# Attention output products of the first 128 tokens moved behind a recurrence, and two chunks' products interleaved

## What is computed

```python
def rwkv7_scan(r, w, k, v, a, b):
    # S_t = S_{t-1} diag(w_t) + (S_{t-1} a_t) b_t^T + v_t k_t^T ; y_t = S_t r_t
...
def rwkv7_mixer(...):
    y = rwkv7_scan(r_h, w_h, k_h, v_h, -kk, kk * a_h)
    mean = jnp.mean(y, axis=-1, keepdims=True)
    var = jnp.mean(jnp.square(y - mean), axis=-1, keepdims=True)
    y = ((y - mean) * lax.rsqrt(var + GN_EPS)).reshape(B_, T_, RW_DIM) * ln_w + ln_b
    return (y + bonus.reshape(B_, T_, RW_DIM)) * g

def second_block(x, ...):
    p = rms_norm_2(x, norm_mix_w) @ w_in
    y_mix = jnp.concatenate([rwkv7_mixer(...), fox_mixer(...)], axis=-1)
    x = x + y_mix @ w_out
    return x + hierarchical_moe(rms_norm_2(x, norm_ffn_w), ...)
```

## Time and profile before

| | |
|---|---|
| median of 3 runs | 1439.1 us (1437.99 to 1439.76) |
| the profiled execution, its own time | 1438.01 us |
| its span, first to last instruction | 1435.8 us |
| granted TensorE clock, mean | 0.906 of full speed |
| PE busy | 1078.6 us, 75% |
| DVE busy | 342.6 us, 24% |
| ACT busy | 217.7 us, 15% |
| POOL busy | 65.5 us, 5% |
| HBM read | 461.45 MB |

### The profile page before, as it was taken

How to read it: one execution, slowest core, us unless ns; L and a number is a source line. 1 busy time by engine, 2 the same in 40 slices (tenths; PEclk the granted TensorE clock), 3 DMA queues, 4 the chain that set the end, 5 groups by cost and what they waited for, 6 DMA issues and landing times.

```text
span 1435.8 us, 34660 instructions
## 1 busy us (share of the span) xinstructions
PE 1078.6 (75%) x15426; PEld 774.4 (54%) x15426; DVE 342.6 (24%) x973; ACT 217.7 (15%) x598; POOL 65.5 (5%) x115
## 2 busy tenths in 40 slices
PE   6999999999999798756566656656566656566665
PEld 4776577646887577544444444444444444444443
DVE  2564156312663451111010111111111101111111
ACT  1163116301432121100000000000000000000000
POOL 1100010001011100000000000000000000000000
PEclk9999999999999899988888898898898887888888
DMA  9752245133220499999999999999999999999997
GB/s 287 257 186 72 91 160 192 31 134 118 78 100 4 177 382 428 428 430 430 431 430 430 430 430 430 430 431 431 430 430 431 429 430 430 430 430 430 431 429 319
DMA packets 69024, 463.37 MB, mean 323 GB/s; under 512 B 14789, under 2 KB 18278, under 8 KB 44390
## 3 DMA queue, kind: packets, MB, share of 16 engines
q1 hardware_dynamic: 64784, 459.77, 77.7%
q10 hardware_dynamic: 4182, 2.74, 0.7%
HBM read 461.45 MB, written 1.05 MB: 322 GB/s over the span
## 4 chain that ended last, share of the span: by engine, by line
DMA 54%; PE 9%; issue 1%; ACT 0%; DVE 0%; POOLq 0%; DVEq 0%; POOL 0%
DMA work_region<-in_exp_w_down_dram 54%; PE bank L2464 5%; PE bank L2455 2%; PE bank L2445 1%; PE bank L2481 1%; PE bank L2417 0%; PE bank L2433 0%; ACT work_region L2382 0%; DVE tokens L2650 0%; POOLq L2333 0%; PE bank L2472 0%; ACT work_region L2378 0%; DVE work_region L2628 0%; DVEq L2651 0%; PE bank L2422 0%
## 5 line engine op out<-in xcount | busy, mean ns | idle before, releaser
L2455 PE MATMUL bank<-weight_slots,work_region 128*32 128x128 f32 x5120 | 190.7, 311 | 124.5 <-DMA weight_slots<-in_exp_w_up_dram 101.5
L2455 PEld LDWEIGHTS bank<-weight_slots,work_region 128*32 128x32 f32 x5120 | 163.5, 125 | 152.4 <-DMA weight_slots<-in_exp_w_up_dram 112.0
L2464 PE MATMUL bank<-weight_slots,work_region 128*32 128x256 f32 x1376 | 112.3, 479 | 87.1 <-DMA weight_slots<-in_exp_w_down_dram 83.8
L2455 PE MATMUL bank<-work_region 128*32 128x128 f32 x2560 | 92.7, 306 | 63.8 <-DMA work_region<-in_exp_w_up_dram 52.5
L2464 PEld LDWEIGHTS bank<-weight_slots,work_region 128*32 128x32 f32 x1376 | 58.1, 132 | 129.1 <-issue 86.8
L2455 PEld LDWEIGHTS bank<-work_region 128*32 128x32 f32 x2560 | 79.3, 123 | 77.8 <-DMA work_region<-in_exp_w_up_dram 57.6
L2382 ACT COPY work_region<-bank 128x256 f32<-128x256 f32 x64 | 23.8, 372 | 604.1 <-PE bank L2464 604.1
L2617 DVE TENSOR_SCALAR work_region<-work_region 128x128 f32<-128x128 f32 x128 | 38.5, 345 | 273.2 <-PE bank L2472 273.2
L543 PE MATMUL bank<-weight_slots,normed_features 128*128 128x512 f32 (+2 forms) x288 | 99.6, 503 | 1.6 <-DVE normed_features L817 1.6
L2628 DVE TENSOR_TENSOR work_region<-work_region,bank 128x128 f32<-128x128 f32 x64 | 23.9, 373 | 291.6 <-PE bank L2455 291.6
L2464 PE MATMUL bank<-work_region 128*32 128x256 f32 x672 | 56.6, 494 | 42.1 <-DMA work_region<-in_exp_w_down_dram 42.1
(11 more groups left out here) (437 smaller groups left out, 1208.7 us busy)
## 6 DMA issues: line engine op xcount, KB each, us to landing
weight_slots<-in_exp_w_gate_dram SPq DMA_DIRECT2D x43, 2048.0 KB, 41.5
weight_slots<-in_exp_w_up_dram SPq DMA_DIRECT2D x43, 2048.0 KB, 40.5
weight_slots<-in_exp_w_down_dram SPq DMA_DIRECT2D x43, 2048.0 KB, 40.5
work_region<-in_exp_w_gate_dram SPq DMA_DIRECT2D x21, 2048.0 KB, 41.6
work_region<-in_exp_w_up_dram SPq DMA_DIRECT2D x21, 2048.0 KB, 40.9
work_region<-in_exp_w_down_dram SPq DMA_DIRECT2D x21, 2048.0 KB, 40.5
weight_slots<-in_w_in_dram SPq DMA_DIRECT2D x16, 2048.0 KB, 10.5
weight_slots<-in_w_out_dram SPq DMA_DIRECT2D x6, 2048.0 KB, 7.9
```

What stands on the lines that cost most here:

```text
L2455: mm = nc.tensor.matmul(B[bank][BLK * j:BLK * (j + 1), 0:P], x[:, c], w[u][:, c, j * P:(j + 1) * P], start=c == 0, stop=c == KC - 1, tile_ ...
L2464: mm = nc.tensor.matmul(B[7][BLK * j:BLK * (j + 1), 0:256], hidt[u][:, BLK * k:BLK * (k + 1)], w_down[u][:, k, j * 256:(j + 1) * 256], sta ...
```

## The change

- **Attention's share.** FO0 and FO1 (tile 0) are no items any more. What they were, eight products (16 records), is made at the end of the mixer in `OUT_BANK[0]`, where tile 0's recurrence share is accumulated on top (`out_fox`, `out_rwkv` with `first` false). FO2 moves up: its first half stands where FO0's second half stood, its second half where FO1's second half stood. FO3 stays. `fox_out(0)` and `fox_out(1)` are gone; `fox_out(2)` stands where `fox_out(1)` stood.
- **Chunks.** `chunk_products` takes several chunks and interleaves them product by product: chunks 0 and 1 together, chunk 2 alone. `y_of_keys(0)` moves behind chunk 2, `step_state(1)` ahead of `turn_writes(1)`. ACT takes h of chunks 0 and 1 behind one count and takes WT1 last.
- **The end.** PE waits for `y_var` 1 and makes `out_fox(0, 0)`, turns tile 0, makes `out_fox(0, 1)`, then the recurrence's share of tile 0, with the turning of tile 1 set inside, then tile 1. DVE does `centre(1)` ahead of `normed(0)`.

The diff, with the core of each piece:

```diff
@@ -1159,8 +1159,8 @@
...
     of_tile = lambda t, m: t[:, m * NH:(m + 1) * NH]
-    ITEMS = """TA0:0 TA1:1 AR0:2 AR1:3 AR2:4 AR3:5 TV0:6 TV1:7 P20:0 P21:1 FO0:6 P40:0 P41:1 KR0:7 KR1:2 P80:4 P81:5 KR2:6 KR3:0 TK0:1 TK1:7 FO1:3
-        G40:2 G41:4 MV0:5 MV1:6 FO2:3 Q0:0 Q1:1 TB0:7 TB1:2 F50:4 F51:5 FO3:6 BONUS:3 XQ0:0 XQ1:7 GA0:1 GA1:2 WU0:5 WV0:6 WU1:0 WV1:3
+    ITEMS = """TA0:0 TA1:1 AR0:2 AR1:3 AR2:4 AR3:5 TV0:6 TV1:7 P20:0 P21:1 P40:0 P41:1 KR0:7 KR1:2 P80:4 P81:5 KR2:6 KR3:0 TK0:1 TK1:7 FO2:3
+        G40:2 G41:4 MV0:5 MV1:6 Q0:0 Q1:1 TB0:7 TB1:2 F50:4 F51:5 FO3:6 BONUS:3 XQ0:0 XQ1:7 GA0:1 GA1:2 WU0:5 WV0:6 WU1:0 WV1:3
         WT0:7 WT1:4""".split()
@@ -1404,16 +1404,15 @@
...
             for q in range(NCH - 1):
-                if q == 1:
+                if q == 2:
                     take(wt[:, 0], "WT0", CT, P)
-                if q == 2:
-                    take(wt[:, 1], "WT1", CT, P)
-                act.wait_ge(S["chunk_made"], q + 1)
+                act.wait_ge(S["chunk_made"], 1 if q < 2 else 2)
                 h_out = view(B[CHUNK_BANK[q]][:, 256:512], CT, HD)
...
                     nc.scalar.copy(chunks[:, q, 1], h_out).then_inc(S["h_taken"], 1)
+            take(wt[:, 1], "WT1", CT, P)
             for m in range(MT):
@@ -1698,15 +1697,12 @@
...
                 of_blocks(f"P2{m}", NT[:, m], N[:, m])
-                if m == 0:
-                    fox_first(0)
-            fox_last(0)
+            fox_first(2)
             for m in range(MT):
...
             of_keys(0)
-            fox_first(1)
             for m in range(MT):
@@ -1715,16 +1711,14 @@
...
             turn("TK1", ei, 1)
-            fox_last(1)
+            fox_last(2)
             for m in range(MT):
...
                 of_blocks(f"G4{m}", P8T[:, m], G[:, m])
-            fox_first(2)
             for m in range(MT):
...
                 of_spans(f"MV{m}", AKT[:, m], view(vtok[:, m], NH, HD))
-            fox_last(2)
             for m in range(MT):
@@ -1790,16 +1784,20 @@
...
 
-            def chunk_products(q):
-                m, s = q // 2, span[q % 2]
+            def chunk_products(some):
                 for h, i, u in HEADS:
                     cols = slice(h * HD, (h + 1) * HD)
-                    out = B[CHUNK_BANK[q]][half[u], :]
-                    g_out, h_out = out[:, i * HD:(i + 1) * HD], out[:, 256 + i * HD:256 + (i + 1) * HD]
-                    if q > 0:
-                        nc.tensor.matmul(g_out, wu[s, m, 0, h], btok[s, m, cols], start=True, stop=True)
-                    nc.tensor.matmul(h_out, btok[s, m, cols], wu[s, m, 1, h], start=True, stop=False)
-                    mm = nc.tensor.matmul(h_out, ktok[s, m, cols], vtok[s, m, cols], start=False, stop=True)
+                    for product in range(3):
+                        for q in some:
+                            m, s = q // 2, span[q % 2]
+                            out = B[CHUNK_BANK[q]][half[u], :]
+                            g_out, h_out = out[:, i * HD:(i + 1) * HD], out[:, 256 + i * HD:256 + (i + 1) * HD]
+                            if product == 0 and q > 0:
+                                nc.tensor.matmul(g_out, wu[s, m, 0, h], btok[s, m, cols], start=True, stop=True)
+                            elif product == 1:
+                                nc.tensor.matmul(h_out, btok[s, m, cols], wu[s, m, 1, h], start=True, stop=False)
+                            elif product == 2:
+                                mm = nc.tensor.matmul(h_out, ktok[s, m, cols], vtok[s, m, cols], start=False, stop=True)
                 mm.then_inc(S["chunk_made"], 1)
@@ -1843,17 +1841,16 @@
...
 
+            needs("TB0", "TK0", "WU0", "WV0")
+            chunk_products((0, 1))
+            turn_writes(0)
+            needs("TB1", "TK1", "WU1", "WV1")
+            chunk_products((2,))
             needs("KR3", "GA0", "GA1")
             y_of_keys(0)
-            needs("TB0", "TK0", "WU0", "WV0")
-            chunk_products(0)
-            turn_writes(0)
-            chunk_products(1)
-            needs("TB1", "TK1", "WU1", "WV1")
-            chunk_products(2)
+            step_state(1)
             turn_writes(1)
             needs("WT0")
-            step_state(1)
             pe.wait_ge(S["h_taken"], 1)
@@ -1872,17 +1869,35 @@
...
             y_of_writes(1)
-            for m in range(MT):
+
+            def turn_y(m):
                 pe.wait_ge(S["y_ready"], m + 1)
...
                 t.then_inc(S["y_transposed"], 1)
-                pe.wait_ge(S["yrt_ready"], m + 1)
-                for h in range(2):
-                    for k in range(4):
-                        mm = nc.tensor.matmul(B[OUT_BANK[m][h]][:, :], yrt[:, k, m * P:(m + 1) * P], w_out[h][:, k, :], start=k == 0, stop=k == 3)
-                    mm.then_inc(S["out_done"], 1)
+
+            def out_fox(m, h):
+                for k in range(4):
+                    nc.tensor.matmul(B[OUT_BANK[m][h]][:, :], yft[:, k, m * P:(m + 1) * P], w_out[h][:, 4 + k, :], start=k == 0, stop=False)
+
+            def out_rwkv(m, h, ks, first):
+                for k in ks:
+                    mm = nc.tensor.matmul(B[OUT_BANK[m][h]][:, :], yrt[:, k, m * P:(m + 1) * P], w_out[h][:, k, :], start=first and k == 0, stop=k == 3)
+                return mm
+
+            pe.wait_ge(S["y_var"], 1)
+            out_fox(0, 0)
+            turn_y(0)
+            out_fox(0, 1)
+            pe.wait_ge(S["yrt_ready"], 1)
+            out_rwkv(0, 0, range(4), False).then_inc(S["out_done"], 1)
+            out_rwkv(0, 1, range(2), False)
+            turn_y(1)
+            out_rwkv(0, 1, range(2, 4), False).then_inc(S["out_done"], 1)
+            pe.wait_ge(S["yrt_ready"], 2)
+            for h in range(2):
+                out_rwkv(1, h, range(4), True).then_inc(S["out_done"], 1)
             w_route = router_memory(mem)[0]
@@ -2056,7 +2071,6 @@
...
                 V.transpose(flat(NO[:, m]), flat(NOT[:, m])).then_inc(S["n_turned"], 1)
-            fox_out(0)
             dve.wait_ge(S["g_ready"], 1)
@@ -2071,14 +2085,13 @@
...
             read_keys(1)
-            fox_out(1)
+            fox_out(2)
             for m in range(MT):
...
                 V.transpose(flat(F[:, m]), flat(G[:, m])).then_inc(S["f_turned"], 1)
-            fox_out(2)
             for m in range(MT):
@@ -2095,7 +2108,7 @@
...
             def take_g(q):
-                dve.wait_ge(S["chunk_made"], q + 1)
+                dve.wait_ge(S["chunk_made"], q)
                 dve.wait_ge(S["decay_ready"], q)
@@ -2156,8 +2169,8 @@
...
             variance(0)
+            centre(1)
             normed(0)
-            centre(1)
             gate_y(0)
```

## The result

The changed kernel takes 1435.8 us (median of 22 runs, 1432.0 to 1438.9) against 1438.7 of before (22 runs): a ratio of 0.9978, 95% interval 0.9971 to 0.9985. It is 3.0 us faster, where 10.2 were forecast and the range began at 6.8. The profiled execution took 1433.85 us, 1431.7 of it span.

The account below looks back on a forecast made before the run. PE's row was taken to bound the middle, and the weight stream's restart at the third count to set the end. Gains 7.6 + 1.1 + 1.5 = 10.2 us, so 1439.1 - 10.2 = 1428.9; range 1426.8 to 1432.3.

Parts of the forecast that it names:

- No wait takes the place, and I take 7.6: Middle: four attention pieces leave PE's row, said to be the bound there; gain 7.6 us, bounds 6.5 to 7.7.
- the removed pieces were covers: Middle, rival: DVE or ACT come late at three or four items, 3 us of 7.6 stay as waits; 1431.9, chance 0.12.
- 0.9 and 0.7 us of spare: Middle: how much earlier DVE's results were laid out to be ready than PE needs them, at P8 and Q.
- the chunks: Recurrence: chunks 0 and 1 merged at 24 ns a record, and a 0.38 wait gone; gain 1.1 us, 0.4 to 1.6.
- the end: Mixer's end: added attention products fill PE's waits, third count of output products comes 1.5 us earlier, 1.2 to 1.8.
- the 0.1 kept back for gaps: Mixer's end: some 0.1 us lost between groups, taken from 1.6 to give the end's 1.5.
- The clock of the end: Mixer's end, rival: PE's clock falls there, costing 2.9 us or half; time 1430.4 to 1431.8, chance 0.25.
- the stream: Behind the mixer: weight stream restarts at count 3 and moves the end equally, at 430 GB/s; rival of no effect, 0.04.

Follow-up runs that it names:

- fox_only: Changed kernel with chunks left one after the other: only attention pieces moved, and the new end; 0.9990 of before, 64.68 us from first turning to y's early loads.
- after: The changed kernel itself, all parts of the change against the kernel before; ratio 0.9978, and 62.82 us from first turning to y's early loads.
- fox_2nd: Second profile of fox_only, nothing changed against it; one run, 65.52 us from first turning to y's early loads.
- merge_only: Kernel before with only chunks 0 and 1 interleaved and the reordering that belongs to it; ratio to before 0.9979.
- after_2nd: Second profile of the changed kernel, nothing changed against it; one run, 63.67 us from first turning to y's early loads.
- small_more: Changed kernel with the small products of item P20 made nine times, 256 products of 32 x 32 more; 1.0078 of before.
- long_one: Changed kernel with eight idle long products at one place, ahead of fox_first(2); 1.0003 of before.
- long_back: Changed kernel with eight idle long products, 7.7 us, put back where the four removed pieces stood; 0.9979 of before.
- after_warm: Changed kernel with three idle products of 256 columns in PE's wait ahead of the last y_of_writes; 0.9982 of before.
- tail_warm: tail_new with idle products in PE's waits of the normalization; 0.9954 of before, and 0.9955 when run again.
- tail_new: merge_only with the end's new order alone, attention products left in the middle; 0.9967 of before.

## Why the prediction was wrong

- **Wrong: "They stand on PE's row, which is the bound there, so the gain counts in full as far as no wait lay under them", and "No wait takes the place, and I take 7.6".** `fox_only` measured 0.0 on it (64.68 against 64.72), and its second profile 0.8 the wrong way: up to the turnings behind the powers the new waits took 5.9 of the 7.7, and the rest went behind them, 1.4 of it in one row at the lower clock. A row without gaps is not yet a row whose length is set by what it executes: in these blocks execution and fetch took nearly the same time. The packets of instructions were 3.7 to 3.9 us apart before, in the stretch 423 to 438 where the items are smallest; in none of the fourteen profiles do two come closer than 3.36, and in the powers of `after` not closer than 3.45. That left a few tenths of a microsecond in each block, and 1.8 us is all that `fox_only` was ahead behind the powers. (By the pace alone the four pieces' 32 instructions are worth 0.4 us, 32/256 of 3.5.) The rows showed it in part: the wait of 1.0 us with the releaser "issue" stood in the powers of before, cutting item P20 behind 24 records. I had left it aside because it was small and would stay.
- **Right in kind, wrong in its place: the rival "the removed pieces were covers".** I had looked for what DVE and ACT would deliver late, found 0.9 and 0.7 us of spare, and both held: no wait of PE in the powers is at P8 or Q for DVE. The only one for DVE is 0.20 us, in `fox_only` and `fox_2nd`, ahead of FO2's first piece, which had moved up; I had put that at nothing. What was covered was the supply of instructions. The rival's price, 3 us of 7.6, was too small as well: 5.0 us of new waits in brackets (5.9 from start to start) and, in most executions, 3.4 to 6.8 us at the lower clock, which cost 1.4 in `after` (4.95 against 3.56 in one row).
- **Right, too small: the chunks.** 1.1 forecast with bounds 0.4 to 1.6; 1.6 in `merge_only`, 1.7 as the mean of the five merged profiles with the pieces kept. The merge itself went to 21 ns where I took 24, near to the state reads' 17. The Trainium skill's rule on row groups ("TensorE: Matmul & The Clock Gate", section "The mechanism") would have given 1.6 in all, which is what was measured; but that a chunk alone ran at 32 ns because of the row group isn't shown: no run changes the halves and nothing else. Against the supply speaks that 128 such records would last 4.1 us, more than the blocks' 3.5, and that no "issue" wait stands in these rows.
- **Right in kind: the end.** 1.5 forecast, bounds 1.2 to 1.8; 2.4 measured against before, 1.4 against `merge_only`. The waits closed as laid out. In the layout count 3 came 19.6 us behind y (502.0 against 482.39), measured are 18.86. The mis-sized terms are a record of 512 columns at 7.13/16 = 0.446 us, and a turning at 0.60: both are lengths of rows, whose modelled ends overlap the next row. From start to start a record takes 0.43 (5.15 for 12, from 488.23 to 493.38), the two turnings 0.49 and 0.43. Together that is 0.7 to 0.8; the 0.1 kept back for gaps wasn't needed.
- **The clock of the end, mostly as forecast.** Of the profiles with the changed kernel's end and nothing in its waits, five have it full through the end (`after`, `after_2nd`, `fox_only`, `small_more`, `long_one`) and two have 3.4 us low (`fox_2nd`, `long_back`): 20.1 instead of 18.86, a price of 1.3 where the rival said 1.4 to 2.9. Its chance of 0.25 fits two in seven.
- **Right: the stream.** 10.53 to 10.58 us from count 3 to the barrier's load in all profiles, and 426 to 432 GB/s in the slices behind it, but for the last (319 before: the forecast's "to the end" passed over it). The instant of the restart moves the end, though not to the tenth: from the restart to the last instruction it is 932.07 us before and 932.2 to 933.3 in the other thirteen profiles.
- **Profiles against run times.** From the first turning to count 3 the four profiles of `after` and `after_warm` average 82.0 against 86.0 of the one of before: 4.0 us, and 3.0 were measured (2.6 for `after_warm`, by its ratio). Of the difference, 0.7 lies behind count 3, where the same four average 932.75 and before has the least of all, 932.07. Part of the runs' spread lies ahead of all this: the first turning stands at 417.5 to 418.0 in six profiles and at 419.0 to 420.8 in eight, with nothing changed ahead of it. The pages part the same way in the second and third slice (36 to 108 us): 256 to 261 and 178 to 191 GB/s in the six, 225 to 242 and 203 to 221 in the eight. So the difference arises there, in the first layers. What sets it, and whether it makes the two groups of run times, stays open.

## What to carry over

Before long work is moved out from between small products, count the instructions: where 256 of them take little more than the 3.5 us seen here, most of what is removed turns into waits for the next block, and gains come from stretches whose blocks last longer. A wait with the releaser "issue" that cuts an item in two, 256 instructions from the next, is the sign of it, even if it is small; there long work, spread between the small products, cost next to nothing here (`long_back`: 7.7 us of it, y 0.13 later). And one profile of each kernel isn't enough where the clock changes level: the end of before, unchanged in `merge_only`, was 1.0 us shorter there.

## What the runs showed of the hardware

- PE's instructions came in packets of 16 KB, 256 instructions, and blocks of 64 small f32 products that execute in 1.28 us started 3.73 us apart (`small_more`); in the fourteen profiles no two packets lie closer than 3.36. A f32 product is four PE instructions: 256 products more brought four packets more.
- The fetch didn't run far ahead: around 7.13 us of long products at one place two packets lie 7.7 us apart. They took away 2.8 of 6.0 us of waits, and in four places 5.0.
- Behind such waits the granted clock fell to its lower level in 5 of 6 profiles, for 3.4 or 6.8 us, and in none of 6 without them, also under rows in which PE was busy throughout (456 to 460 in `after`). The same kernel did it at another place, or not at all, in another execution.
- Idle products in PE's waits of the end: the clock full in both profiles of `tail_warm`, low for 6.8 us in `tail_new`, and 16.5 us against 18.9 to count 3.
